# Gathers that leave out empty slots in the expert stage of a two-layer decoder trunk

## The reference, cut to what matters

```python
def hier_moe(h, wg, bg, we, be, w1, w3, w2):
    # top-1 of 4 groups, then top-2 of the 4 experts inside it
    ...
    expert_id = g_idx[:, None] * MOE_EXPERTS_PER_GROUP + top_i
    combine = jnp.sum(jax.nn.one_hot(expert_id, MOE_EXPERTS, dtype=jnp.float32) * top_w[..., None], axis=1)
    for e in range(MOE_EXPERTS):
        he = jax.nn.silu(t @ w1[e]) * (t @ w3[e])
        out = out + combine[:, e:e + 1] * (he @ w2[e])
```

```
layer 0: 53 61 52 52 86 80 79 65 68 85 65 68 46 49 57 58
layer 1: 64 49 62 57 69 57 53 65 96 73 57 66 62 68 62 64
```

## Time and profile before

| | us |
|---|---|
| median of three runs | 1661.14 |
| lowest and highest run | 1660.94, 1664.81 |
| the profiled execution, its own time | 1661.2 |
| its span, first to last instruction | 1659.3 |
| PE busy (share of the span) | 1487.0 (90%) |
| DVE busy | 629.2 (38%) |
| ACT busy | 376.1 (23%) |
| POOL busy | 188.8 (11%) |

### The profile page before, as it was taken

The page is one execution under the profiler, slowest core; times in us unless marked ns, Lnnn a source line. Parts: engine busy times, 40 slices in busy tenths (PEclk is TensorE's granted clock), DMA queues, the critical chain, the costliest instruction groups (busy, mean ns, idle before and its releaser), DMA issues. The chain is left out here.

```text
span 1659.3 us, 26238 instructions
## 1 busy us (share of the span) xinstructions
PE 1487.0 (90%) x10732; PEld 780.8 (47%) x10732; DVE 629.2 (38%) x1263; ACT 376.1 (23%) x708; POOL 188.8 (11%) x205
## 2 busy tenths in 40 slices
PE   6999999979799799998848999899999979999882
PEld 3444444467544443433323444448998545343331
DVE  4420400056400561311259159462847446131125
ACT  2012111123400111111135057323332111111112
POOL 0001000006100010100020014210132001001002
PEclk9999999989899899999979999997999989999996
DMA  5423422002011699999943202100002419999996
GB/s 190 152 102 131 165 80 80 0 8 95 1 51 51 239 390 409 417 412 416 418 150 151 78 23 70 58 0 2 27 2 103 177 39 399 413 416 414 417 416 221
DMA packets 72644, 306.38 MB, mean 185 GB/s; under 512 B 7488, under 2 KB 9664, under 8 KB 47616
## 3 DMA queue, kind: packets, MB, share of 16 engines
q1 hardware_dynamic: 57808, 264.78, 40.4%
q0 software_dynamic: 8928, 30.68, 5.0%
q10 hardware_dynamic: 5840, 9.96, 1.7%
HBM read 303.30 MB, written 27.26 MB: 199 GB/s over the span
## 5 line engine op out<-in xcount | busy, mean ns | idle before, releaser
L1224 PE MATMUL bank<-arena 128*32 128x512 f32 x2048 | 236.8, 604 | 24.6 <-DMA arena<-in_moe_w 23.7
L505 PE MATMUL bank<-arena 128*128 128x512 f32 x512 | 222.1, 593 | 0.0
L1640 PE MATMUL bank<-arena 128*128 128x512 f32 (+1 forms) x448 | 193.1, 602 | 1.4 <-ACT arena L1743 1.4
L505 PEld LDWEIGHTS bank<-arena 128*128 128x128 f32 x512 | 96.4, 190 | 117.5 <-issue 117.5
L1507 DVE TENSOR_TENSOR arena<-arena,bank 64x512 f32<-64x512 f32 x32 | 22.1, 691 | 324.2 <-ACT arena L1289 324.2
L1224 PEld LDWEIGHTS bank<-arena 128*32 128x32 f32 x2048 | 65.7, 111 | 159.1 <-issue 119.5
L1640 PEld LDWEIGHTS bank<-arena 128*128 128x128 f32 (+1 forms) x448 | 83.7, 192 | 103.3 <-issue 98.2
L1539 POOL DMA_INDIRECT arena<-token_rows,index x54 | 52.4, 970 | 698.0 <-DVE index L1367 436.6
L1256 PE MATMUL bank<-arena 128*32 128x512 f32 x1024 | 116.5, 595 | 0.0
L974 PE MATMUL bank<-arena 128*128 128x512 f32 x256 | 110.5, 593 | 1.5 <-ACT arena L996 1.5
L502 PE MATMUL bank<-arena 128*128 128x512 f32 x192 | 82.6, 593 | 2.1 <-PEq L350 2.1
(11 more groups left out here) (389 smaller groups left out, 1948.0 us busy)
## 6 DMA issues: line engine op xcount, KB each, us to landing
arena<-in_moe_w SPq DMA_DIRECT2D x216, 1024.0 KB
arena<-in_w_in_e SPq DMA_DIRECT2D x11, 2048.0 KB, 9.0
slot_rows<-zero POOLq DMA_DIRECT2D x20, 512.0 KB, 8.1
arena<-in_w_out_e SPq DMA_DIRECT2D x4, 2048.0 KB, 8.6
slot_rows<-arena ACTq DMA_DIRECT2D x64, 128.0 KB, 8.2
token_rows<-arena SPq DMA_DIRECT2D x8, 512.0 KB, 11.9
arena<-in_rw_wr SPq DMA_DIRECT2D x2, 2048.0 KB, 13.0
arena<-in_rw_wk SPq DMA_DIRECT2D x2, 2048.0 KB, 8.5
```

The costliest lines, as they stand in the source:

```text
L505: mm = nc.tensor.matmul(bank[:, 0:width], ut[:, kk, m * P:(m + 1) * P], w[:, kk, 0:width], start=kk == 0, stop=kk == KD - 1)
L1224: mm = nc.tensor.matmul(bank[H[s]][band * BAND:(band + 1) * BAND, :], xt[:, kk, half, s * BAND:(s + 1) * BAND], b["w13"][:, e, k, w * FF:( ...
L1640: mm = nc.tensor.matmul(t.bank[i % BANKS][0:rows, :], left, right, start=n == 0, stop=n == len(pairs) - 1)
```

## The change

The row numbers are moved up, so that an empty slot's number lies behind the table's last row: `row_of` loses 1024 and `row_half` gains 1024. The sum for a filled slot is what it was, and for an empty slot it is 1024 or 1025. The gathers get a bound of 1023 and leave out what lies behind it. A place that is left out keeps what it held, so POOL writes zeros to the three destinations at the beginning of each stage. The kernel has the same instructions otherwise, in the same order on every engine; lines from L1068 on move down by one, and those behind the new memsets by six.

```diff
-    row_half = np.stack([i >= P // 2, i >= P // 2, i >= P // 4], 1)
-    row_of = 2 * (np.arange(NT)[None, :] * P + i[:, None])
+    row_half = 2 * SEQ + np.stack([i >= P // 2, i >= P // 2, i >= P // 4], 1)
+    row_of = 2 * (np.arange(NT)[None, :] * P + i[:, None]) - 2 * SEQ
...
+        s_blank = sem("rows_blank")
...
             def gather(x, at, n):
                 return nc.gpsimd.indirect_dma_start(out=x, out_offset=None, in_=halves,
-                                                    in_offset=bass.IndirectOffsetOnAxis(ap=t.index[0:n, at:at + 1], axis=0))
+                                                    in_offset=bass.IndirectOffsetOnAxis(ap=t.index[0:n, at:at + 1], axis=0),
+                                                    bounds_check=2 * SEQ - 1, oob_is_err=False)
...
+            nc.gpsimd.memset(b["xa"][:, 0, :], 0.0).then_inc(s_blank, 1)
+            nc.gpsimd.memset(b["xa"][0:PAIR, 1, :], 0.0).then_inc(s_blank, 1)
+            nc.gpsimd.memset(b["xb"], 0.0).then_inc(s_blank, 1)
+            pool.wait_ge(s_blank, 3)
             pool.wait_ge(t.s_clear, 16 * XG_TILES)
             pool.wait_ge(t.s_rows[layer], 16 * NT)
             pool.wait_ge(s_index_a, 2)
```

## The result

The changed kernel takes 1656.42 us (median of 19 runs, 1652.53 to 1659.96), the kernel before 1662.81 us beside it (19 runs). The ratio is 0.9955 with a 95% interval of 0.9948 to 0.9963. So it is 0.45% faster, 7.5 us, with an interval of 6.2 to 8.6 us. I had forecast 2.8 us and called that no change. The time lies in the range of 1653.5 to 1663.0, but the sign of the effect is clear and its size is above my forecast and above the full count of 5.9 us.

A forecast was written before the change was run, and what follows sets the result against it. The prediction took the transfer stream to bound both expert stages. It subtracted 2.8 us (1.4 and 1.3 for the engine saving least), all other terms taken as zero, from 1661.2 to reach 1658.4 us; range 1653.5 to 1663.0.

The forecast's parts named there:

- full count: Rival for both expert stages: left-out rows cost nothing, the rest is spread evenly; 5.9 us saved, 1655.3 us, chance 0.26.
- The bound of the kernel: Both expert stages: the transfer stream, all 16 DMA engines busy at 415 GB/s, sets the pace; bytes removed come back in full.
- The number of rows: Gathers for visits 1 to 8: empty slots amount to 674 half rows in layer 0 and 530 in layer 1.
- Fixed blocks with the slowest engine in charge: Gathers: each DMA engine serves fixed partitions, and the one saving least sets the gain, 2.8 us in all.
- plain count: Both expert stages: every left-out half row saves 4.9 ns and all DMA engines gain alike, 5.9 us at most.
- least-relieved engine: The DMA engine of the first slots, saving only 18 half rows in layer 0 and 17 in layer 1; 2.8 us.
- The slower pace near gathers: Stream beside gathers and stores, 399 against 426 GB/s: fewer rows might gain at most 1.6 us; taken as nothing.
- Memsets, bound, last set: Stage start, gathers and stage end: three POOL memsets, the index check and a smaller last set, each taken as 0.
- better pace: Faster stream near gathers with fewer rows, at most 1.6 us over 16 sets; with the full count, 1653.7 us.
- signs of being wrong: Stage shorter by more than 4 us, DMA bytes unchanged, or the last gather coming to release the combine.
- Nothing saved: Rival for the gathers: empty slots still cost as much, only memsets remain; 1661.2 us, up to 1664.4, chance 0.23.
- longer gathers: Rival for POOL's last three gathers before the combine: the bound makes gathers longer; 1666.7 us, chance 0.08.

The follow-up runs named there:

- e9: The changed kernel with no row gathered at all in layer 1; ratio to the kernel before 0.9897, layer 1 stage 264.1 us.
- e5: The changed kernel, also leaving out rows for partitions 64 to 127 of the two large gathers in layer 1; ratio to the kernel before 0.9952.
- e7: The changed kernel with slots dealt out so that neighbouring partitions hold slots 16 apart (8 in the small gather); ratio to the kernel before 0.9950.
- e12: The changed kernel with slots spread over the partitions, the same edit as e7 measured again on another chip; 1652.09 us, ratio 0.9935.
- e2: The kernel before, without bound or memsets, each empty slot reading a distinct half row; ratio to the kernel before 1.0018.
- e1: The changed kernel with bound and memsets, but empty slots keep row 0 or 1, so all rows move; ratio to the kernel before 0.9998.

## Why the prediction was right or wrong

**The bound of the kernel: right, but for the set of visit 1.** Rows taken from the stream evenly came back: 12.5 us for 12.6 in e9. The set of visit 1, which I counted among those that compete with weights, is fetched in layer 1 at a DMA share of 0.94, and leaving it out lowered the share instead.

**The number of rows: right.** 3.04 MB less, by the queue's own count, and a left-out row is nearly free: 4 bytes, and 9 ns for a packet of two.

**Fixed blocks with the slowest engine in charge: right as a mechanism, its price in this change not confirmed.** The mechanism is shown by e5 against the change and by the half share at the stream's end. The Trainium skill, *DMA: Bandwidth & Descriptors*, section "The descriptor swizzle", which was weighed against the plain count, agrees with e5's half share: for a plain transfer of 1 MiB to 128 partitions it gives partitions 64 to 127 to eight engines of their own. Which partitions exactly make a block was not tried. The 18 and 17 rows of the least-relieved engine also need to know who serves the 64 partitions of the small gather, and neither a row nor a run shows that.

By my forecast the blocks held back 5.9 - 2.8 = 3.1 us. Spreading the slots, which should have given back 1.7 us or more, gave 0.8 us in the stages, and in the totals between nothing clear (e7) and 4 us (e12).

**The size: too small, 2.8 us forecast and 7.5 measured.** The step that failed for certain is "The slower pace near gathers", where I wrote "I take nothing". I had put it at 1.6 us at most, in proportion to the rows. The windows show a faster pace in both stages, worth up to 3.5 us, and it isn't in proportion: it is as large with the change's rows left out as with none gathered.

What the rest is stays open between two sums. One is the least-relieved engine and the pace, 2.8 + 3.5 = 6.3 us. The other is the count without the sets of visit 1 and the pace. Visit 1 has 19 and 46 empty slots, 130 of the 1204 half rows, so this is 1074 x 4.9 ns = 5.3 us and 3.5, together 8.8 us. The totals give 7.5 us (6.2 to 8.6), between the two; the stages give 8.4, near the second. If the second holds, the step that takes 2.8 us instead of 5.9 failed too, and the blocks cost this change a few tenths of a us.

What makes the pace rise is not settled. It isn't the many reads of one row (e2, in the form tried), nor the bound or the memsets (e1), and the spread of the places doesn't change it (e7 runs at 419 GB/s, the change at 418).

**Memsets, bound, last set: right**, each cost nothing that the runs can tell (e1, the timeline).

**The rivals.** The full count (0.26) was closest by number, 1655.3 us, and with the better pace, 1653.7, it is 7.5 us below 1661.2, just what was measured. Its sign also came: the share stayed at 1.02 and the last `w13` landed 3.3 us earlier after the barrier. Its reason, that what remains is dealt out evenly, is refuted by e5; in this change the difference was small. Of my signs of being wrong, a stage shorter by more than 4 us is met in layer 0 (4.6 by the means) and nearly in layer 1 (3.8). Nothing saved, and longer gathers, did not occur; a gather is longer by 0.055 us.

**The chances.** Faster by over 0.3% had 0.28. I had taken a known direction (fewer bytes in a full stream), priced at its lower end, and set a term of known sign to zero. Both leaned the same way. That the time lies in my range is partly luck: its low end came from the full count with better pace, not from the sum that I believed.

## What to carry to other kernels

When a stage runs at the pace of its transfers, count what moves without use: padding rows, and sets fetched for a turn that never comes. Bytes removed evenly from all DMA engines came back nearly one for one (e9). Bytes removed from half of them, by the partitions that they go to, came back not at all (e5), so look at the share in the last microseconds of the stream and spread what is left out over the partitions.

An experiment that leaves out data must not change what later steps do with it; here a router downstream added a visit. And where single runs spread by more than the effect, the length of the stage within a profile tells where the time went; but it is one execution, so several profiles are needed, and the total beside them.

## What the runs showed of the hardware that I had not expected

A row behind the bound keeps its place in its packet, with 4 bytes in place of 2048: 72644 packets before and after, 728 of them with 8 bytes instead of 4096. Leaving out 1204 of 5120 half rows made the saturated stream 0.7% faster (415 to 418 GB/s), and leaving out all rows of a layer made it no faster than that. In e5, where eight DMA engines had less to do, the share of the middle gave no sign of it; it showed only in the last 8 us.
